# Byte offsets of the weight and moving tiles in SBUF, in a two-block kernel on one core

## The reference

```
# block 1
h = rms_norm(x, g_mix);  proj = h @ w_in              # 2048 x 9216 + gates
y_a = stick_breaking_attention(q, k, v) @ w_oa;  y_b = spatial_gating(u, v) @ w_ob
x = x + (sigmoid(gate_a) * y_a + sigmoid(gate_b) * y_b) @ w_out
x = x + square(relu(rms_norm(x, g_ff) @ w_ff1)) @ w_ff2          # 2048 x 8192 x 2048
# block 2
mod = silu(c) @ ada_w + ada_b                          # scales and shifts, also for ctx
p = modulate(rmsnorm(x)) @ w_in_2;  kc, vc = modulate(rmsnorm(ctx)) @ w_in_2[:, keys and values]
y = [neighbourhood_attention, fourier_mix, hyena_mix](p);  x = x + g1 * (y @ w_out_2)
x = x + g2 * (gelu(dwconv(gate)) * up) @ w_down        # gate, up = modulate(rmsnorm(x)) @ w_up
return rmsnorm(x, final_norm_g)
```

## The kernel before

| tiles | bytes past a multiple of 128 |
|---|---|
| RAW | 0 |
| WH, WL | 32 |
| X, XH, XL, HH, HL, NT; other tiles that share their places (t1, hSD, Ef, fU, ...) | 64 |
| MH, ML, CH, CL and the rest of the area that begins at AR | 96 |

## Time and profile before

### The profile page before, as it was taken

One profiled execution on the slowest core, in us unless ns is written; L12 is line 12 of the kernel. 1 busy time (PEld: TensorE's weight loads), 2 busy tenths in 40 slices (PEclk: granted clock), 3 DMA queues, 4 the chain that ended last, 5 costly groups with the idle time before them and its releaser, 6 DMA issues. The chain is left out here.

```text
span 2727.9 us, 50263 instructions
## 1 busy us (share of the span) xinstructions
PE 2665.3 (98%) x21116; PEld 2574.7 (94%) x21116; DVE 1899.0 (70%) x2409; ACT 1178.1 (43%) x1228; POOL 0.2 (0%) x4
## 2 busy tenths in 40 slices
PE   7999999998999999999999999999899999999998
PEld 7988999998999999999999899958899999999998
DVE  7778877886898787878883235756666666666666
ACT  4666554433544444444442233324444444444443
POOL 0000000000000000000000000000000000000000
PEclk9999999999999999999999999999999999999999
DMA  8666667665888888888763254422455555555552
GB/s 285 219 226 216 215 225 244 242 238 183 271 264 277 276 277 276 276 277 276 265 223 109 93 155 130 133 84 93 155 186 186 186 187 192 192 186 186 186 191 103
DMA packets 282681, 558.27 MB, mean 205 GB/s; under 512 B 10407, under 2 KB 16840, under 8 KB 282056
## 3 DMA queue, kind: packets, MB, share of 16 engines
q1 hardware_dynamic: 282104, 553.60, 60.4%
q10 hardware_dynamic: 400, 2.11, 0.3%
HBM read 553.57 MB, written 2.10 MB: 204 GB/s over the span
## 5 line engine op out<-in xcount | busy, mean ns | idle before, releaser
L475 ACT ACTIVATE WH<-RAW 128x1024 fp32r<-128x1024 f32 x840 | 890.6, 1063 | 1375.9 <-PE PS L1584 1251.8
L879 DVE TENSOR_TENSOR WL<-RAW,WH 128x1024 fp32r<-128x1024 f32 x840 | 1018.8, 1222 | 667.6 <-ACT WH L475 657.9
L1584 PE MATMUL PS<-XH,WH 128*128 128x256 f32 x4288 | 687.9, 282 | 22.9 <-issue 9.8
L1584 PE MATMUL PS<-XL,WH 128*128 128x256 f32 x4288 | 678.0, 280 | 0.0
L1584 PE MATMUL PS<-XH,WL 128*128 128x256 f32 x4288 | 677.6, 280 | 0.0
L1584 PEld LDWEIGHTS PS<-XH,WH 128*128 128x128 f32 x4288 | 581.8, 189 | 28.5 <-issue 14.8
L1584 PEld LDWEIGHTS PS<-XL,WH 128*128 128x128 f32 x4288 | 578.9, 189 | 0.0
L1584 PEld LDWEIGHTS PS<-XH,WL 128*128 128x128 f32 x4288 | 578.7, 189 | 0.0
L1584 PE MATMUL PS<-HH,WH 128*128 128x256 f32 x1728 | 272.4, 279 | 0.4 <-DVE X L1189 0.4
L1584 PE MATMUL PS<-HL,WH 128*128 128x256 f32 x1728 | 271.9, 279 | 0.0
L1584 PE MATMUL PS<-HH,WL 128*128 128x256 f32 x1728 | 271.9, 279 | 0.0
(11 more groups left out here) (240 smaller groups left out, 1704.7 us busy)
## 6 DMA issues: line engine op xcount, KB each, us to landing
RAW<-in_w_ff SPq DMA_DIRECT2D x128, 1024.0 KB, 5.5
RAW<-in_w_in SPq DMA_DIRECT2D x112, 1024.0 KB, 5.2
RAW<-in_w_up SPq DMA_DIRECT2D x88, 1024.0 KB, 5.0
adab<-in_ada_w SPq DMA_DIRECT2D x128, 512.0 KB, 4.6
RAW<-in_w_down SPq DMA_DIRECT2D x44, 1024.0 KB, 5.0
ada1b<-in_ada_w SPq DMA_DIRECT2D x64, 512.0 KB, 6.0
RAW<-in_w_out SPq DMA_DIRECT2D x32, 1024.0 KB, 5.1
RAW<-in_w_oa SPq DMA_DIRECT2D x8, 1024.0 KB, 5.2
```

Source lines behind the costliest of these rows:

```text
L475: A(WH[:, c.base % 2, hs], RAW[:, c.base % SLOTS, hs], ACT.Copy).then_inc(hi_done, 1)
L879: tt(WL[:, b, hs], RAW[:, c.base % SLOTS, hs], WH[:, b, hs].bitcast(f32), ALU.subtract)\
L1584: ins = MM(out[:, f, :], w[:, b, kk, f * P:(f + 1) * P], x, start=first and n == 0 and f % 2 == 0, stop=last and n == 2, skip_group_check= ...
```

## The change

All tiles get new offsets. No instruction is added, removed or moved: the sequence of each of the five engines is the same, row for row, apart from line numbers that are 8 higher.

| tiles | before | after |
|---|---|---|
| WH, WL | 32 | 0 |
| X | 64 | 0 |
| XH, XL, NT, t1, hSD, Ef, fU and others in their places | 64 | 96 |
| MH, ML and the area at AR | 96 | 96 |
| HH / HL | 64 / 64 | 56 / 60 |
| CH / CL | 96 / 96 | 112 / 120 |

`HH`, `HL`, `CH` and `CL` get their places through a longer tile whose first few words are skipped, since a tile itself starts at a multiple of 32 bytes.

```
-        WH = at("WH", [P, 2, FT, NB], 32 * K + 32, f32r)
-        WL = at("WL", [P, 2, FT, NB], 48 * K + 32, f32r)
-        X = at("X", [P, KC, T], 64 * K + 64)
-        XH = at("XH", [P, KC, T], 80 * K + 64, f32r)
-        XL = at("XL", [P, KC, T], 96 * K + 64, f32r)
-        HH = at("HH", [P, 2, FT, T], 112 * K + 64, f32r)
-        HL = at("HL", [P, 2, FT, T], 120 * K + 64, f32r)
-        NT = at("NT", [P, KC, T], 112 * K + 64)
-        CON = 128 * K + 64
+        WH = at("WH", [P, 2, FT, NB], 32 * K, f32r)
+        WL = at("WL", [P, 2, FT, NB], 48 * K, f32r)
+        X = at("X", [P, KC, T], 64 * K)
+        XH = at("XH", [P, KC, T], 80 * K + 96, f32r)
+        XL = at("XL", [P, KC, T], 96 * K + 96, f32r)
+        def hidden_half(name, offset, skip):
+            t = at(name, [P, skip + 2 * FT * T], offset, f32r)
+            return t[:, skip:].rearrange("p (b f t) -> p b f t", b=2, f=FT)
+
+        HH = hidden_half("HH", 112 * K + 128 + 32, 6)
+        HL = hidden_half("HL", 120 * K + 128 + 32, 7)
+        NT = at("NT", [P, KC, T], 112 * K + 96)
+        CON = 128 * K + 192
...
-        t1 = 112 * K + 64
+        t1 = 112 * K + 96
...
+        def context_half(name, offset, skip):
+            t = at(name, [P, skip + KC * T], offset, f32r)
+            return t[:, skip:].rearrange("p (k t) -> p k t", k=KC)
...
-        CH = at("CH", [P, KC, T], AR + 40 * K, f32r)
-        CL = at("CL", [P, KC, T], AR + 56 * K, f32r)
+        CH = context_half("CH", AR + 40 * K, 4)
+        CL = context_half("CL", AR + 56 * K, 6)
...
-        hSD = at("hSD", [P, 2, 2, TT, HW], 80 * K + 64)
-        Ef = at("Ef", [P, TT, 6 * P], 104 * K + 64)
+        hSD = at("hSD", [P, 2, 2, TT, HW], 80 * K + 96)
+        Ef = at("Ef", [P, TT, 6 * P], 104 * K + 96)
```

More of the change, by code:

```diff
@@ L245, in build_program @@
         SM = at("SM", [P, KC, T], AR + 8 * K)
-        fcl = at("fcl", [P, TT, 2 * T], 80 * K + 64)
-        fcd = at("fcd", [P, 2, P], 84 * K + 64)
-        fU = at("fU", [P, FNG, 2 * T], 88 * K + 64)
+        fcl = at("fcl", [P, TT, 2 * T], 80 * K + 96)
+        fcd = at("fcd", [P, 2, P], 84 * K + 96)
+        fU = at("fU", [P, FNG, 2 * T], 88 * K + 96)
         KS = at("KS", [P, 2, 5, HW], AR + 24 * K)
@@ L251, in build_program @@
         YS = at("YS", [P, 4, HW], AR + 48 * K)
-        hSD = at("hSD", [P, 2, 2, TT, HW], 80 * K + 64)
-        dec = at("dec", [P, 2, TT, HW], 96 * K + 64)
-        Ef = at("Ef", [P, TT, 6 * P], 104 * K + 64)
-        pz = at("pz", [33, T], 110 * K + 64)
-        w1h = at("w1h", [33, 64], 111 * K + 64)
-        w2h = at("w2h", [64, 64], 111 * K + 64 + 512)
+        hSD = at("hSD", [P, 2, 2, TT, HW], 80 * K + 96)
+        dec = at("dec", [P, 2, TT, HW], 96 * K + 96)
+        Ef = at("Ef", [P, TT, 6 * P], 104 * K + 96)
+        pz = at("pz", [33, T], 110 * K + 96)
+        w1h = at("w1h", [33, 64], 111 * K + 96)
+        w2h = at("w2h", [64, 64], 111 * K + 96 + 512)
         w3h = at("w3h", [64, 2048], t1)
```

## The result

The changed kernel is slower. Its median is 2791.56 us (2791.28 to 2794.48, 4 runs) against 2735.18 us of the kernel before on the same chip; the ratio is 1.0203, with a 95% interval of 1.0174 to 1.0231. The forecast was 2690 us, and the time lies outside its range of 2640 to 2755.

The account below looks back on a forecast made before the run. The prediction took PE's matmul cadence as the bound and summed -42.5 us (X in `ws`) and -2.8 us (X in `tok`) to -45.3 us, all else 0, forecasting 2690 us from a median of 2734.87, range 2640 to 2755.

Parts of the forecast that it names:

- What bounds the kernel: PE, busy 98% of the span, sets the pace; only the time per matmul matters, 1 ns being 18.0 us.
- step 1: XH, XL in `ws`, (32, 64) to (0, 96): 116.6 to 113.25 ns, -42.5 us; ends -64 and +15 us.
- step 3: HH, HL moved to (0, 56) and (0, 60): 0; ends -17.1 and +6.2 us.
- rival C: X and H all fall into the slow 117.8 ns pattern: +21.7 us, 2757 us; chance 17%.
- Step 2: XH, XL in `tok`, (64, 32) to (96, 0): -2.8 us; ends 0 and twice that.
- Step 4: MH, ML, (32, 96) to (0, 96): same mixture of patterns, 0; ends -2.6 and +0.8 us.
- Step 5: CH, CL moved to (0, 112) and (0, 120): 0; +2.1 us if they fell to the X cadence.
- Steps 6 and 7: Plain float32 matmuls on tiles moved from 64 to 96, and ACT and DVE writes at new offsets: 0 each.
- Can the others keep up: DVE (to 86%) and DMA (to 285 GB/s) in the first feed-forward network keep room; nothing taken off.
- Rival A: Only the distance between operands counts: X stays at 116.6 ns, H gains 17.1 us; 2720 us, chance 18%.
- Rival B: Nothing changes: offsets only move the phase between loads and matmuls, same mixture of patterns; 2735 us, chance 15%.
- Rival D: X and H both reach the bound of weight loads alone: -90 us, 2645 us; chance 10%.

Follow-up runs that it names:

- the tables: Kernels of matmuls alone over many pairs of weight and moving places, one in steps of 16 bytes, one of 4: 272 to 296 cycles a matmul.
- e7: Changed kernel with XH, XL, HH and HL moved to 112, weights left at 0: 2684.62 us, ratio 0.9818 to the kernel before.
- m2: Matmuls alone, 12 pairs of places, each in 12 blocks of 48 begun at different moments: one or two cadences a pair.
- e6: Kernel before with weights at 40 and XH, XL, HH, HL, MH, ML at 80, C still at 96: 2680.01 us, ratio 0.9795.
- the first table: Matmuls alone, eight weight by eight moving places in steps of 16 bytes, plus some between: (0, 96) 288 cycles, (32, 64) 280.
- m6: Matmuls alone, six cases of places, run with ACT and DVE idle and again beside their SBUF traffic: same cadence to 0.1 cycle.
- m5: Matmuls alone with separate high and low tiles, some after a block at X's place: (0, 56 and 60) 285.3 cycles, (0, 60 and 60) 280.1.
- e3: Kernel before with weights at 16 and XH, XL, HH, HL, MH, ML at 80, C still at 96: median 2737.11 us, ratio 1.0018.
- the finer table: Matmuls alone, 512 pairs of places in steps of 4 bytes, two blocks of 36 each: 272 to 296 cycles.

## Why the prediction was wrong

- **What bounds the kernel** was right. PE's cadence is the time: the changes of PE's cadence sum to 66.5 us (65.1 over all starts) and the span moved by 64.8.
- **The change part by part, step 1, is what failed**, in its first choice: "The nearest row by the moving offset is CH at 96, 113.25 ns", and so -42.5 us for X. X at (0, 96) takes 120.0 ns, +43.7 us. Two things were wrong in it. A row at (32, 96) says nothing of (0, 96): the tables and e7 show that neither the weights' place nor the moving one nor their distance decides, but the pair. And 113.25 was one of two patterns of its pair; M had shown the other at the same places, and in m2 it was the usual one, 10 of 12.
- **The upper end of step 1** was wrong with it: 117.8 ns was the slowest pattern that the trace showed, and I took it as the bound. The tables have values up to 296 cycles, 123.3 ns. The same bound, +1.2 ns, stood in step 3 and in rival C, whose sign was right but whose price of 21.7 us was a third of the 60.8 us that X and H lost: they did not fall into the slow pattern of M, 117.8 ns, but into one of 120.0 that no row before had. The range did not even hold C's own figure, 2757 us, though C had a chance of 17%; its upper end of 2755 was too low by the prediction's own working.
- **Step 2** (`tok`): -2.8 us forecast, +0.6 us measured. **Step 3** (H): 0 forecast, +17.1 measured. **Step 4** (M): 0 forecast, +2.5. **Step 5** (C): 0 forecast; +2.6 measured with both forms, where the end was +2.1.
- **Steps 6 and 7** held. The chain of the changed kernel has the same 16 records of L1945 in 6.87 us, as before, and DVE's and ACT's busy times moved by 0.1 and 0.2%.
- **Can the others keep up:** not tested by the change, which made PE slower; in e6, at the forecast cadence, they did but for some 5 us: PE waits 4.9 us for DVE's X, where it was 1.6, and 6.7 us for `WL`, where it was 5.3.
- **Three slips** in the prediction's numbers, without weight for the outcome: of the 6336 matmuls of the last piece only 4224 are on X, so X alone would have made it 13.9 us shorter and not some 20. And the offset was not worth 3.3 ns "in both forms": in `tok` it was 4.1 ns of 233.3, which is 2.1 ns per 256 columns. The "16 matmuls" of step 6 are 8 in the source: each plain float32 matmul leaves two records, here of 429 ns each.
- **Rival A** falls as a law, by the diagonals of the first table. **Rival B** had a true core: the start does pick between patterns, but only between those of the pair. **Rival D** was put at 2645 us; the fastest pattern of any pair tried is 272 cycles, and the kernel that has it for X, H and M takes 2680 us. The figure of the Trainium skill (TensorE: Matmul & The Clock Gate, section on the back-to-back issue gap), which the page gives for an isolated matmul and which makes an estimate of 109.2 ns for 256 columns, was not reached by any of the 512 pairs; the lowest is 113.3 ns.
- The rule of the Trainium skill that PE's two read ports are independent and PE waits on no one (SBUF — State Buffer, section on who interferes with whom) has two halves here. That PE does not wait on ACT and DVE agrees with m6. That the place of one operand against the other is worth nothing does not: 113.3 to 123.3 ns with PE alone on the core.

**Open.** H takes 288.0 cycles in the changed kernel and 285.3 in m5 with the same two places, and with both halves at 60 it takes 286.9 in the kernel and 280.1 in m5. What runs ahead (m5) and SBUF traffic of ACT and DVE (m6) were tried and are not it. The amount of DMA traffic does not show either: in the changed kernel H takes 288.0 cycles in the first feed-forward network, with the DMA engines at 266 GB/s, and 287.9 in the second, at 183. DMA traffic against none, reads of PSUM, the bank of PSUM and the alternation of the two weight buffers were not tried. The difference in the changed kernel is 5184 x 2.7 cycles, 5.8 of the 64.8 us. Nor is it shown what in the hardware makes the patterns: the tables describe them and the kernels confirm that they carry over, no more.

## What to carry to other kernels

Where PE is the bound and float32r matmuls follow each other without waits, the byte places of the stationary and the moving tile are worth several per cent as a pair. Measure the pair by itself, with a dozen starts at different moments, and take one that has only its fast pattern; (40, 80) and (0, 112) did here. Do not carry a cadence from one pair to another, and where one row of a trace shows two cadences for the same instructions, take neither as a bound.

## What the runs showed of the hardware that was not expected

- With PE alone on the core at 2.4 GHz, a 256-column float32r matmul with its own weight load takes 272 to 296 cycles, by the places of the two operands in SBUF.
- The cadence locks in: from 12 or 16 starts a pair showed one to three values, each held over the rest of a block in the small kernels and over hundreds of microseconds in e3. In the finer table 288, 282.7 and 280 cycles are the most frequent, and 272 is rare (17 of 1024 blocks). An interruption can move PE to another value of the pair. This gives one program several times: 2718.73 to 2748.12 us for e3.
- A moving tile 4 or 8 bytes past a multiple of 16 is dearer on average (290.7 and 288.6 cycles) than one at 0 or 12 (283.6 and 281.7); for the weights' place the four means lie within 0.9 cycles. The Trainium skill (SBUF — State Buffer, section Specifications (TRN2)) gives SBUF lines of 16 bytes; the trace agrees as far as the means of the moving side have a period of 16 bytes (the four means are 284.0, 290.7, 288.3 and 282.3 in the even and 283.1, 290.6, 288.8 and 281.1 in the odd 16 bytes), and no run here shows by what mechanism.
- ACT at 93% and DVE at 98% on other places of SBUF changed the cadence by at most 0.1 cycle in 30 blocks (m6).
